# Writing expert results back: one fp32 copy, double-buffered, in place of a high and a low half

## What is computed

```python
hid = silu(einsum('btd,edf->btef', h, w_exp_gate)) * einsum('btd,edf->btef', h, w_exp_up)
routed = einsum('btef,efd->btd', hid * gate[..., None], w_exp_down)   # 8 of 64 experts per token
out = routed + shared
```

## Time and profile before

| | |
|---|---|
| median of three runs | 1038.51 us |
| profiled execution | 1035.76 us, of it the core's span 1033.9 us |
| mean granted clock | 0.943 |
| PE busy | 937.7 us, 91% of the span |
| VectorE busy | 407.0 us, 39% |
| ScalarE busy | 189.4 us, 18% |
| chain that ended last | PE 79%, VectorE 9%, DMA 5% |
| DMA | 298.71 MB, 289 GB/s over the span |

### The profile page before, as it was taken

The page is one execution under the profiler, slowest core; times in us unless marked ns, Lnnn a source line. Parts: engine busy times, 40 slices in busy tenths (PEclk is TensorE's granted clock), DMA queues, the critical chain, the costliest instruction groups (busy, mean ns, idle before and its releaser), DMA issues.

```text
span 1033.9 us, 13518 instructions
## 1 busy us (share of the span) xinstructions
PE 937.7 (91%) x5432; PEld 553.8 (54%) x5432; DVE 407.0 (39%) x900; ACT 189.4 (18%) x333; POOL 64.0 (6%) x62
## 2 busy tenths in 40 slices
PE   2899699888999977999999999999999999998982
PEld 0586386444554446655555555555555555545650
DVE  2121775666535195033333433333333333332125
ACT  1222421011121121211111111111111111111111
POOL 0000233334100000000000000000000000000000
PEclk8699989999999986999999999999999999997777
DMA  8944415554760872799999999999999999955550
GB/s 292 358 159 156 163 63 180 187 213 174 265 215 10 325 292 87 287 410 415 417 396 404 404 393 406 401 400 404 401 396 401 409 390 410 416 198 196 218 206 41
DMA packets 79562, 298.71 MB, mean 289 GB/s; under 512 B 9200, under 2 KB 11248, under 8 KB 61328
## 3 DMA queue, kind: packets, MB, share of 16 engines
q1 hardware_dynamic: 75440, 289.14, 71.9%
q0 software_dynamic: 2144, 5.84, 1.7%
q10 hardware_dynamic: 1920, 2.92, 0.8%
HBM read 296.27 MB, written 1.61 MB: 288 GB/s over the span
## 4 chain that ended last, share of the span: by engine, by line
PE 79%; DVE 9%; DMA 5%; ACT 2%; issue 2%; POOL 1%; PEldq 0%; DVEq 0%; SPq 0%; ACTq 0%; PEld 0%
PE bank L1611 24%; PE bank L1649 13%; PE bank L1637 7%; PE bank L1367 6%; PE bank L1601 6%; PE bank L1374 4%; DMA ring<-in_w_ada 3%; PE bank L1493 3%; PE bank L1624 2%; PE bank L1508 2%; PE bank L1675 2%; DVE lev_e L1001 2%; PE bank L1390 2%; PE bank L1519 1%; PE bank L1347 1%
## 5 line engine op out<-in xcount | busy, mean ns | idle before, releaser
L1611 PE MATMUL bank<-ring,x_g 128*64 128x256 f32 x1728 | 204.6, 391 | 2.7 <-ACT x_g L854 2.6
L1611 PEld LDWEIGHTS bank<-ring,x_g 128*64 128x64 f32 x1728 | 129.3, 142 | 90.0 <-issue 38.6
L1649 PE MATMUL bank<-down_w,hid_t 128*64 128x512 f32 x560 | 135.6, 605 | 0.0
L1374 PE MATMUL bank<-ring,h_t 128*128 128x512 f32 x256 | 112.9, 594 | 2.0 <-issue 2.0
L1242 DVE COPY hid_t<-bank 128x128 f32<-128x128 f32 x70 | 20.4, 292 | 219.4 <-PE bank L1626 219.4
L1266 DVE TENSOR_TENSOR y_lo<-bank,y_hi 128x512 fp32r<-128x512 f32 x70 | 48.4, 691 | 135.1 <-ACT y_hi L836 135.1
L1374 PEld LDWEIGHTS bank<-ring,h_t 128*128 128x128 f32 x256 | 47.4, 190 | 61.7 <-issue 61.7
L836 ACT ACTIVATE y_hi<-bank 128x512 fp32r<-128x512 f32 x70 | 41.8, 597 | 179.6 <-PE bank L1649 179.6
L1649 PEld LDWEIGHTS bank<-down_w,hid_t 128*64 128x64 f32 x560 | 33.9, 136 | 65.2 <-issue 65.2
L1367 PE MATMUL bank<-h_t,ring 128*128 128x256 f32 x288 | 65.6, 389 | 2.3 <-DVE h_t L932 1.8
L1637 PE MATMUL bank<-y_hi,put_back 64*128 64x512 f32 x280 | 62.6, 443 | 2.8 <-DVE y_lo L1266 2.8
(11 more groups left out here) (229 smaller groups left out, 964.0 us busy)
## 6 DMA issues: line engine op xcount, KB each, us to landing
down_w<-in_w_exp_down SPq DMA_DIRECT2D x70, 1024.0 KB, 7.9
ring<-in_w_exp_gate SPq DMA_DIRECT2D x54, 1024.0 KB, 7.2
ring<-in_w_exp_up SPq DMA_DIRECT2D x54, 1024.0 KB, 9.4
ring<-in_w_in SPq DMA_DIRECT2D x13, 2048.0 KB, 9.0
ring<-in_w_ada SPq DMA_DIRECT2D x12, 2048.0 KB, 9.8
up_more<-in_w_exp_gate SPq DMA_DIRECT2D x16, 1024.0 KB, 7.2
up_more<-in_w_exp_up SPq DMA_DIRECT2D x16, 1024.0 KB, 9.4
ring<-in_w_out SPq DMA_DIRECT2D x2, 2048.0 KB, 10.2
```

What stands on the lines that cost most here:

```text
L1374: ins = mm(out[:, :], h_t[:, k, tok(h)], w[:, k, :], start=k == 0, stop=k == KD - 1)
L1611: ins = mm(gu_bank[h * SLOTS:(h + 1) * SLOTS, 0:2 * P].rearrange("p (b n) -> p b n", b=2), x[:, k, :], up_w[slot][:, :, k, h * P:(h + 1) * ...
L1649: ins = mm(y_bank[h * SLOTS:(h + 1) * SLOTS, :], hid_t[:, f * SLOTS:(f + 1) * SLOTS], down_w[:, slot, f, h * BANK:(h + 1) * BANK], start=f ...
```

## The change

`y_hi` and `y_lo` go. ScalarE makes one plain fp32 copy `y` with two buffers, even and odd items (`y_out`); the copy of item n waits for the scatter of item n-2 where `y_high` waited for that of item n-1. VectorE's subtraction `y_low` is gone. `put_back` becomes plain fp32, and `scatter` has four plain fp32 products where it had eight fp32r products. `scatter` and `down` wait for `y_ready`, which ScalarE raises.

```diff
-        y_hi = moe("y_hi", [P, BANK], F32R)
-        y_lo = moe("y_lo", [P, BANK], F32R)
+        y = moe("y", [P, 2, BANK])
...
-        put_back = moe("put_back", [P, 2, G, P], F32R)
+        put_back = moe("put_back", [P, 2, G, P])
...
-            def y_high(n):
+            def y_out(n, odd):
 
                 act.wait_ge(down_done, val(n + 1))
-                need(scattered, n)
-                nc.scalar.activation(y_hi[:, :], y_bank[:, :], ACT.Copy).then_inc(y_hi_ready, 1)
+                need(scattered, n - 1)
+                nc.scalar.activation(y[:, odd], y_bank[:, :], ACT.Copy).then_inc(y_ready, 1)
...
-            def y_low(n):
-
-                dve.wait_ge(y_hi_ready, val(n + 1))
-                nc.vector.tensor_tensor(y_lo[:, :], y_bank[:, :], y_hi[:, :].bitcast(F32), ALU.subtract).then_inc(y_lo_ready, 1)
...
                     put_backs(n, q)
-                    y_low(n - 1)
...
                 pe.wait_ge(put_back_ready, val(n + 1))
-                pe.wait_ge(y_lo_ready, val(n + 1))
+                pe.wait_ge(y_ready, val(n + 1))
                 for g in range(G):
-                    for y in (y_hi, y_lo):
-                        for h in range(2):
-                            rows = slice(h * SLOTS, (h + 1) * SLOTS)
-                            ins = mm(acc_bank[2 * g + h][:, :], put_back[rows, odd, g, :], y[rows, :], start=False, stop=True,
-                                     tile_position=(h * SLOTS, 0), skip_group_check=True)
+                    for h in range(2):
+                        rows = slice(h * SLOTS, (h + 1) * SLOTS)
+                        ins = mm(acc_bank[2 * g + h][:, :], put_back[rows, odd, g, :], y[rows, odd, :], start=False, stop=True,
+                                 tile_position=(h * SLOTS, 0), skip_group_check=True)
```

More of the change, by code:

```diff
@@ L451, in hybrid_layer @@
         silu_ready, hid_ready, hid_t_ready = sem("silu_ready"), sem("hid_ready"), sem("hid_t_ready")
-        y_hi_ready, y_lo_ready, scattered = sem("y_hi_ready"), sem("y_lo_ready"), sem("scattered")
+        y_ready, scattered = sem("y_ready"), sem("scattered")
         moe_done, out_ready, out_stored = sem("moe_done"), sem("out_ready"), sem("out_stored")
@@ L848, in _ @@
                 if n:
-                    y_high(n - 1)
+                    y_out(n - 1, (n - 1) % 2)
             turns = more_turns(act)
@@ L858, in _ @@
                     silu(n)
-                    y_high(n - 1)
-            y_high(Count(turns, MORE_PER_TURN, N_EXP - 1))
+                    y_out(n - 1, (q + 1) % 2)
+            y_out(Count(turns, MORE_PER_TURN, N_EXP - 1), 1)
             for n in range(6, 8):
@@ L1279, in _ @@
                     picks(n // ITEMS_PER_TURN + 2)
-                if n:
-                    y_low(n - 1)
             turns = more_turns(dve)
@@ L1299, in _ @@
                     put_backs(n, q)
-                    y_low(n - 1)
             n_items = Count(turns, MORE_PER_TURN, N_EXP)
             hidden_turned(n_items - 1)
-            y_low(n_items - 1)
             dve.wait_ge(moe_done, 1)
@@ L1645, in down @@
                 pe.wait_ge(hid_t_ready, val(n + 1))
-                need(y_lo_ready, n)
+                need(y_ready, n)
                 for f in range(2):
```

## The result

The changed kernel is slower: median 1074.11 us (1067.63 to 1076.15, four runs) against 1037.04 us, ratio 1.0345, 95% interval 1.0286 to 1.0404. Run again beside other kernels it came to 1.0374 (1.0343 to 1.0404). The forecast was 1067 us, the range 1056 to 1099.

What follows compares the result with a forecast made beforehand. PE's own work was taken to bound the items. Scatters +55.1 us, waits for `pick` -5.8, clock -17.4, tail 0 gave +31.9 us on 1035.8: 1067.7, stated as 1067 us; range 1056 to 1099.

Steps and rivals of the forecast that it cites:

- the falling clock: Rival, loop turns: the granted clock still falls in each turn, so only 5.8 us come back; 1085 us; chance 0.24.
- the stagger: Rival, scatter: only neighbouring instructions of different halves overlap, five steps of 0.43 us instead of four; 1098 us; chance 0.09.
- the forecast's own part: Range of the forecast alone: 1056 us (scatter's lower bound) to 1073 us (one fall of the clock); chance 0.52.
- the step on the clock: Loop turns: without PE's wait for `pick` the clock stays at the upper level, saving 5.8 us a turn, 17.4 in three.
- What bounds the kernel: Written-out items: PE's own work sets the pace, 7.86 us per item; savings on VectorE or ScalarE there are worth nothing.
- The scatter's term: Items and loop: each scatter takes 1.94 us against 1.12, 0.81 us more; 68 scatters add 55.1 us.
- The pairing: Scatter: its eight plain fp32 instructions run side by side in four pairs of 0.43 us, as in the down projection.
- The wait for pick: Head of each loop turn: `pick` follows `put_back`, so PE's waits lose 2.2 + 1.8 + 1.8 = 5.8 us.
- The prediction's own signs of being wrong: Five or eight steps per scatter; clock 0.50 in turns; PE waiting for `ring` or `down_w` in items; items still 7.9 us.
- The tail: Last two scatters: some 0.75 us of waiting each goes, each scatter is 0.81 us longer; zero in sum.
- The weights of a turn's second item: Loop turns: they land about 966.1 and a faster turn wants them at 968.1, so 2 us are in hand.

Runs made afterwards that it cites:

- the run with the pick alone: The kernel before with the last `y_low` of a turn moved behind the next turn's `pick`, scatter still eight fp32r products; 1020.19 us, ratio 0.9855.

## Why the prediction was right, and where it was off

- **The number**: 1074.11 us is 7 us over the forecast and inside the range. The range was so wide because it took in the falling clock and the stagger; the forecast's own part of it ended at 1073 us, so the number does not bear out the step on the clock. The four runs of the changed kernel differ by that too: 1067.63 and 1072.76 us at a mean granted clock of 0.966 and 0.967, 1075.45 and 1076.15 us at 0.952 and 0.953.
- **What bounds the kernel**: right. PE sets the pace of an item. The longer scatter went into the time in full (+47.4 us over the 61 scatters of the items' stretch), and the shorter one of the run without `y_lo` came out in full as long as the weights came in time. VectorE's saved 0.69 us per item was worth nothing inside the items: with a subtraction back at its place their stretch took 532.5 us, without it 532.6.
- **The scatter's term**: right. 1.94 us was reckoned for it, 1.92 measured; in the item 0.78 us instead of 0.81, so 47.4 us for 61 scatters where 49.4 stood.
- **The pairing**, taken as given: right. The Trainium skill's rule in "TensorE: Matmul & The Clock Gate" (Part 3) that matmuls start strictly in program order would have made it a stagger; the run with the halves in turn, in pairs from the start, does not fit it if the program's order is the code's.
- **The wait for pick**: right. It is gone in all three turns; the run with the pick alone shows that it, and not the scatter, is the loop's gain. One reading was off: by the prediction's own times `put_back` starts 1.54 us ahead of the down's end (925.25 and 926.79), not 1.7; the sum goes by the times and isn't touched.
- **"I take it that the clock stays up"**: wrong, and the one step that failed. The prediction's own signs of being wrong came: rows at 0.50 in the turns, a first up of 5.35 us instead of 3.6. The evidence was the mixers' waits of up to 1.5 us with no fall. For the mixers it holds: in the changed kernel's two profiles the clock fell there three times, each time behind a wait of 1.84 to 1.96 us, and not behind the others, which are up to 1.4 us long. The first profile has one of the three:

```profile
140.00:370.00 230.00, 214.01 (x836) 118.65 (x835) 121.50 (x189) 36.15 (x53) 50.48 (x47) 0.99 0.51 183
```

```profile
217.43 1.13 PE L1380 MATMUL bank<-lev_q,lev_k 128*128 128x128 f32 x8 [1.96 <-POOL lev_k L620]
```

  What failed was to carry this over to the turns: there, falls stood behind waits of 0.69 and 0.87 us, between short matmuls, if shorter falls than in before. The prediction had noted that the mixers don't show waits in this way. The term was 17.4 us; with the waits' 5.8 and the scatters' +4.9 the loop was to lose 18.3 us, and it lost 11.5 in the profiled execution, 6.8 short. It lies between the forecast and the rival *the clock still falls*, and differs between executions (70.9 and 66.6 us for the same stretch). The doubt was named there, but was left out of the value.
- **The tail**: right within 0.2 us (+0.8 with the scatter left over from the loop, +1.0 measured). The waits behind the last two downs are 1.5 us now, 2.8 before.
- **The weights of a turn's second item** came in time: no wait for them is in the list.
- The rest, 2.8 us, lies ahead of the experts, in code that wasn't touched.

## What to carry to other kernels

Before trading two products in fp32r for one in plain fp32, count instructions and their pace: here a plain product is two instructions, and two such products side by side take 0.86 us where two in fp32r take 0.225. That is nearly four times as much, so a plain product costs nearly twice the two that it replaces, and on a full engine nothing hides that. An operation that looks free by its engine's load can still stand ahead of something urgent in that engine's queue; here moving one subtraction behind the next `pick` gave 1.5%, with none of the change. And price a wait on TensorE with the clock that falls behind it: here that cost nearly twice the wait (11.4 us beside 6.3).

## What the runs showed of the hardware that was not expected

- In the gather of the loop, fp32r products of 128 columns take 0.11 us each at the upper level (0.22 us per row of two, 956.83 to 957.05). In the gather ahead of the items, fp32r products of 512 columns, with a stationary operand of the same 128x128, take 0.23 us each (0.46 us per row of two), as the kernel before shows:

```profile
431.92 0.62 PE L1601 MATMUL bank<-pick,h_hi 128*128 128x512 f32 x2
432.38 0.61 PE L1601 MATMUL bank<-pick,h_lo 128*128 128x512 f32 x2
```

A quarter of the columns takes half the time; why, no run shows.
- Side-by-side pairs formed with either order of the products in the code: 1.92 us per scatter in both.
- The granted clock falls in a turn or doesn't at the same wait of 0.87 us, in the same execution. In the mixers it fell behind waits of 1.84 to 1.96 us in the changed kernel's two profiles, and stayed up behind one of 2.00 us in the profile of the run with the pick alone.
